# A two-layer mixer trunk on eight cores: the norm of a tile begun on its own sums, weight blocks taken one by one, and the residual reloaded over the length of a stage

## What is computed

```python
def reference(x, ...):
    h = x
    for layer in range(2):
        xn = rmsnorm(h, mix_norm_g[layer])
        if layer == 0:
            p = xn @ ab_w_in                       # 1024 -> 2048
            a, xb, gate_b, gate_c = split(p)       # 512 columns each
            a_out = pool_mixer(a, pool_w, pool_scale)        # trailing means 2/4/8/16, minus the token
            b_out = gate_b * short_conv(gate_c * xb, conv_w, conv_b)   # causal, width 3
            mix = concat(a_out, b_out) @ ab_w_out
        else:
            p = xn @ cd_w_in                       # 1024 -> 2560
            u, v = split(gelu(p[..., :1024]))
            c_out = spatial_gating(u, v)           # layernorm(v), W_s per 128-position chunk, times u
            d_out = stick_breaking_attention(q, k, v_of(p))  # 8 heads of 64, strictly causal
            mix = concat(c_out, d_out) @ cd_w_out
        h = h + mix
        hn = rmsnorm(h, mlp_norm_g[layer])
        h = h + square(relu(hn @ mlp_w1[layer])) @ mlp_w2[layer]   # 1024 -> 4096 -> 1024
    return rmsnorm(h, final_norm_g)
```

## Time and profile before

| | us |
|---|---|
| median of 3 runs | 2912.78 (2911.24 to 2913.79) |
| the profiled execution | 2921.03 |
| its span, slowest core (core 6) | 2919.3 |
| spans of the eight cores | 2894.6 to 2919.3 |
| TensorE busy | 2801.1 (96%) |
| ScalarE, VectorE, GpSimd busy | 1527.9, 1395.3, 1286.5 |

### The profile page before, as it was taken

One profiled execution on the slowest core, in us unless ns is written; L12 is line 12 of the kernel. 1 busy time (PEld: TensorE's weight loads), 2 busy tenths in 40 slices (PEclk: granted clock), 3 DMA queues, 4 the chain that ended last, 5 costly groups with the idle time before them and its releaser, 6 DMA issues.

```text
span 2919.3 us, 43744 instructions; the slowest of 8 cores (2894.6 to 2919.3 us)
## 1 busy us (share of the span) xinstructions
PE 2801.1 (96%) x12957; PEld 1252.3 (43%) x13219; DVE 1395.3 (48%) x1706; ACT 1527.9 (52%) x2488; POOL 1286.5 (44%) x1488
## 2 busy tenths in 40 slices
PE   9999889999999999899999999999999989999998
PEld 3444334444444344344444444444444434444443
...
GB/s 166 172 181 183 200 214 79 117 128 139 215 166 139 174 185 164 193 97 144 162 177 162 86 105 118 109 166 163 99 123 123 101 216 131 120 111 180 85 80 87
DMA packets 491478, 420.24 MB, mean 144 GB/s; under 512 B 310128, under 2 KB 334960, under 8 KB 491248
## 3 DMA queue, kind: packets, MB, share of 16 engines
...
q0 software_dynamic: 26064, 47.36, 11.5%
...
...
## 4 chain that ended last, share of the span: by engine, by line
PE 88%; DMA 3%; issue 3%; DVE 2%; ACT 2%; POOL 1%; SPq 0%; DVEq 0%; ACTq 0%; POOLq 0%
PE ps L626 82%; PE ps L1423 4%; PE ps L1479 2%; DMA ring<-wblk 1%; DMA Wk<-Wq 1%; DVE vt L1269 1%; POOL ps L1116 0%; DMA stg<-xT 0%; ACT tmp L614 0%; DVE P L1442 0%; DMA oT<-stg 0%; ACT ps L614 0%; DVE X L802 0%; DVE X L752 0%; DVE h L871 0%
## 5 line engine op out<-in xcount | busy, mean ns | idle before, releaser
L626 PE MATMUL ps<-X,ring 128*128 128x512 bf16 x6016 | 1397.2, 385 | 35.1 <-DMA ring<-wblk 5.9
L626 PEld LDWEIGHTS ps<-X,ring 128*128 128x128 bf16 x6144 | 603.3, 99 | 777.9 <-issue 131.3
L1456 POOL TENSOR_TENSOR Wq<-P 128x1024 bf16<-128x1024 f32 (+2 forms) x320 | 530.2, 1659 | 590.2 <-DVE P L1442 578.9
L1442 DVE TENSOR_TENSOR_SCAN P<-ps,carry,cbs 128x512 f32<-128x512 f32 x384 | 489.1, 1279 | 381.9 <-ACT ps L614 256.8
L626 PE MATMUL ps<-mix,ring 128*128 128x512 bf16 x2752 | 654.6, 381 | 9.0 <-DMA ring<-wblk 2.8
L626 PE MATMUL ps<-ffB,ring 128*128 128x512 bf16 x2008 | 479.9, 379 | 2.1
L871 POOL TENSOR_TENSOR h<-tmp,h 128x512 f32<-128x512 f32 x220 | 287.4, 1307 | 346.1 <-DVE tmp L866 345.1
L866 DVE TENSOR_TENSOR tmp<-ps,ms 128x512 f32<-128x512 f32 x256 | 175.1, 684 | 539.4 <-PE ps L626 530.2
L614 ACT ACTIVATE tmp<-ps 128x512 f32<-128x512 f32 x512 | 303.8, 593 | 239.2 <-PE ps L626 199.0
L626 PEld LDWEIGHTS ps<-mix,ring 128*128 128x128 bf16 x2816 | 274.5, 98 | 340.8 <-issue 29.7
L614 ACT ACTIVATE ps<-ps 128x1024 f32<-128x1024 f32 (+2 forms) x320 | 280.0, 878 | 158.3 <-PE ps L1423 157.6
...
## 6 DMA issues: line engine op xcount, KB each, us to landing
...
```

Source lines behind the costliest of these rows:

```text
L626: ins = pe.matmul(out, lhsT=l, rhs=r, start=(first and i == 0), stop=(last and i == n - 1), skip_group_check=True)
L1442: yield Req("dve", (lambda h: lambda e: e.tensor_tensor_scan(out=P[:, h, 0:w][:, ::-1], data0=zt[:, h * 512:h * 512 + w][:, ::-1], data1=l ...
L1456: yield Req("pool", lambda e: e.tensor_tensor(out=W4, in0=P[:, :, 1:w + 1].rearrange("p h (j n) -> p h j n", n=128), in1=P[:, :, 0:w].rear ...
```

## The change

1. stage_F spawns norm_h of both tiles before the MLP, with bias -2 where it had -0.2; it then waits only for its own tile's sums. The Exp of the norm has a bias of -2.
2. Blocks are taken one by one (or two by two for w2) just ahead of the group of tile 0 that first reads them, in stage_F, out_proj, mlp and for U. U's four blocks come before V's in the order of the ring.
3. The first U group of a tile waits chunk by chunk for X, in the planning too.
4. A chunk's reload of h also waits until 8 + 1.5 x (8 t + c) groups of M have been planned (mg counts them): from group 8 to group 30.5 of the forty.
5. The planning waits for a chunk of h in its evacuation (evac_x), not for all eight ahead of the out-projection.
6. finbusy is waited for before the fourth group of a set (which writes mix) and before the pooling product, not before every group.

```diff
-B_L0IN, B_L0OUT, B_MLP, B_V, B_U, B_VV, B_K, B_Q, B_L1OUT = 0, 16, (24, 116), 88, 92, 96, 100, 104, 108
+B_L0IN, B_L0OUT, B_MLP, B_V, B_U, B_VV, B_K, B_Q, B_L1OUT = 0, 16, (24, 116), 92, 88, 96, 100, 104, 108
...
     def group(self, pairs, reads, evac, fine=None, ok=None):
...
+        self.mg += self.inm
...
+                if ok is not None:
+                    yield ok(i)
...
     def evac_x(self, c, t, ev, gcol, hk):
...
         def evac(bk):
+            yield lambda: c in self.hcount.get(hk, ())
...
     def mlp(self, l, ev, then):
...
-                sl = yield from self.take(8)
+                sl = []
                 for t in range(2):
                     for j in range(8):
+                        if t == 0:
+                            sl += yield from self.take(1)
...
             if q == 1:
                 self.rate = RATE_OUT
-                sl = yield from self.take(8)
+                sl = []
                 for t in range(2):
-                    for c in range(4, 8):
+                    for c in range(8 - TAILC, 8):
+                        if t == 0:
+                            sl += yield from self.take(2)
...
     def chain_pool(self, g, t, p, seq0, tn):
...
+            yield lambda: t not in self.finbusy
             b2 = yield (self.banks,)
...
     def stage_F(self, n, s, u):
...
-            yield lambda: t not in self.finbusy
             if i == 0:
                 yield lambda: (s, u, t) in self.xready
...
             for b in (1, 2, 0, 3):
+                if b == 3:
+                    yield lambda: t not in self.finbusy
...
-        yield from self.mlp(0, ev2, then)
-
         def dst(t):
             f = self.to_X(t, 1)
 
             def g(c, *a):
                 yield from f(c, *a)
-                self.free_h(nx, c, t, lambda: (c, t) in spilled)
+                nd2.add((c, t))
+                self.free_h(nx, c, t, lambda: (c, t) in spilled and self.mg >= 8 + 1.5 * (t * 8 + c))
             return g
         for t in range(2):
-            self.M.spawn(self.norm_h(ev2[t], t, 16, dst(t), nd2), -0.2)
+            self.M.spawn(self.norm_h(ev2[t], t, 16, dst(t), nd2), -2)
+        yield from self.mlp(0, ev2, then)
...
     def stage_M(self, sn, s, u):
...
-        sl = yield from self.take(8)
+        su, sl = [], []
...
-            yield lambda: t in self.nd3
...
+                if t == 0:
+                    su += yield from self.take(1)
+                yield from self.group(self.wpairs(su[g], X, ts), [self.Lring[su[g]]] + ([] if g == 0 else Lx), evac,
+                                      fine=Lx if g == 0 else None, ok=lambda k: lambda: (k, t) in self.nd3)
...
+            if t == 0:
+                sl = yield from self.take(4)
```

46 lines of the change are left out of this document (26 added, 20 removed).

## The result

The changed kernel took 2872.86 us (median of 4 runs, 2870.34 to 2878.92) beside 2913.28 for the kernel before: a ratio of 0.9859, 95% interval 0.9834 to 0.9884, or 40.4 us less. The forecast was 2879, 34 us less. The experiments ran on three other chips (1, 5 and 15), where the kernel before takes 2898, 2897 and 2898 us; a number of runs there are disturbed on one die or both, and only undisturbed ones are used here.

A forecast was written before the change was run, and what follows sets the result against it. TensorE was read as busy 2801.1 of 2919.3 us, leaving idle and slow clock to win. F to M 22.4 plus S boundaries 11.5 made 33.9, say 34 us, from 2912.8 to 2879 us; range 2855 to 2906.

The forecast's parts named there:

- Norm and U, three M stages: Starts of three M stages, tile 0's norm early, U ahead of tile 1's sums: 6.0, 6.8 and 7.1 us gained.
- The table switch: On ScalarE in the early norm: 1.28 us; by the skill's 2.66 us, up to 0.1 us lost at each place.
- the cover: From tile 0's sums on, TensorE has 11.3 us of work while X takes 9.1; cover 1.5 us, queueing costs nothing.
- The sum of idle and clock: At the boundaries, TensorE's idle plus busy time times (1 - clock) counts as lost; the clock part is 20.8 us.
- M(0,0): First M boundary: U begins sooner, V's block brings a wait of 5 us or more; gain put at 4.0 us.
- The burst: At M(0,0), SP's 15 reloads in 16.13 us land while two weight blocks land; spread, they stand aside.
- The chain of V, -1.5: V of tile 0 has two more groups ahead of its norm chain on VectorE: -1.5 us, bounds 0 and -5.3.
- S(0,0) to F(1,0): Three groups of the next stage run before tile 1's sum of squares: 5 us gained, ceiling 7.1, DMA the next bound.
- S to S: At S(0,1) to S(1,0) and S(1,0) to S(1,1), next stage's groups before tile 1's sum: 4 and 2.5 us gained.
- The sign of being wrong: TensorE idles at the S boundaries for L849 or for an output write by as much as before.
- Blocks one by one: nothing: Taking blocks one by one elsewhere than at M(0,0) gains nothing, since the ring is full when a stage begins.
- The other signs: L756 waits under 8 us, X in two runs of 8, no U idle, loads over 60 us, clock over 0.95.

The follow-up runs named there:

- the filler: The kernel before with 12 matmuls of constants put ahead of the four sum matmuls of tile 1's norm of h: ratio 0.9987.

## Why the prediction came out right, and where it did not

*Norm and U, three M stages.* Put at 6.0, 6.8 and 7.1; measured 4.5, 6.9 and 7.3. The order was read rightly, no wait for w2's evacuation shows in the tail, and the clock is back. The table switch costs less than the cover: in the changed kernel the Ln stands 0.01 us behind the load, and the load had waited 0.20:

```profile
1160.66 1.28 ACT L780 ACT_TABLE_LOAD   x1 [0.20 <-PE ps L627]
1161.95 0.69 ACT L780 ACTIVATE ms<-ps,cfs 128x512 f32<-128x512 f32 x1
```

So the extra 1.38 us of drain that the Trainium skill states ("ScalarE: Activation LUTs", "What ACT_TABLE_LOAD costs") shows neither before nor behind this load.

The sum of idle and clock gave the right size for a reason that the prediction did not have. It took 3.5, 4.0 and 3.6 us behind the idle (chunks and clock added); the traces show one cost there, the pace of VectorE's sixteen chunks, 2.9 us, and on some cores 1.7 of low clock behind it. With the idle of 2.46, 2.82 and 3.52 us that makes 5.4, 5.7 and 6.4 us of the measured 4.5, 6.9 and 7.3; differences of about 1 us stay open. It comes back with half of the chunks now written under w2 (the run from 767.48 above). Where the filler kept TensorE busy and the clock at 1.00, and left the chunks as they were, nothing came back. That the terms met the measured time so closely is in part luck.

*The norm as the cause.* The prediction credited the norm's early start; alone it brings nothing that can be told from no change (0.9981, up to 1.0009). The prediction had read the order of the whole change, so its number did not suffer, but its account of what does what did.

*M(0,0).* The new wait came as said, if somewhat smaller (2.6 to 5.3 us, against "5 us or more"), but the term of 4.0 was mis-sized: 9.4. What it left out is the gating's chain. It took the waits there as given and even put 1.5 us on top; in fact the wait of 4.17 us for vn went, since the order with the reloads spread sets the products elsewhere. The burst was seen as a nuisance for two weight blocks; with it back, the whole gain of this stage is gone.

*The chain of V, -1.5.* Not so at the other stages either: eight waits for vt, 7.8 us on core 6 against 6.7 of before, but in no stretch a loss.

*S(0,0) to F(1,0).* 5 put, 4.5 measured, with a wait at a place the prediction did not name: the pooling operand, not an output write.

*S to S.* 6.5 put, 3.6 measured, which is no more than this stretch scatters. The sign of being wrong that the prediction named did come: at S(0,1) to S(1,0) TensorE waits for L849 by more (4.59 and 3.53 us on core 6) than it had waited for L752 (3.77). So the overlap that it counted on, early groups of the next stage under the last norm, gave back most of what it took.

*Blocks one by one: nothing.* Held beside the spread. With them and without the spread U came first at M(1,0), which the early norm alone did not bring.

*The other signs.* The waits for L756 are 4.7 us (under 8), X is written in two runs of eight, U has no idle, the clock is over 0.95 at three M boundaries but 0.91 at M(0,0). The reloads of M(0,0) are spread over 46 us (370.15 to 415.94, core 6), not 60, the first five still in a row.

The errors, measured less put, were +5.4 at M(0,0), +1.5 for the chain, -2.9 at S to S, -1.5 at M(0,1), -0.5 at S to F and +0.3 at the other two: 33.9 against 36.2 by stretches and 40.4 by the medians. That the sum came so near is partly luck: one term was less than half of what it should be, and others made up for it.
